# Two blocks on one core: a new engine order in the first mixer, the low-rank gate on four row groups, and gated linear attention in steps of 128 tokens

## The reference

```python
# layer 0 of the first block: HGRN2 (4 heads of 128, chunks of 32) beside a causal convolution of 31 taps
f = lb + (1.0 - lb) * sigmoid(f_pre);  k = (1.0 - lb) * sigmoid(-f_pre);  log_f = log(f)
b = cumsum(log_f within a chunk);  q_t = q * exp(b);  k_t = k * exp(-b)
o = causal(q_t k_t^T) v + q_t S;  S = exp(b_last) * S + (k * exp(b_last - b))^T v
o = rms_scaled(o) * hg_norm_g * silu(g)
u = silu(layer_norm(conv31(a * sigmoid(a_gate)) + cv_b));  y = [o, u] @ w_out
# layer 0 of the second block: gated linear attention (4 heads, keys 128, values 256, chunks of 64)
gk = log_sigmoid(glr @ w_gk2 + b_gk) / 16.0            # glr: 16 columns of the input projection
bcum = cumsum(gk within a chunk);  q_t = q * exp(bcum);  k_t = k * exp(-bcum)
o = causal(q_t k_t^T) v + q_t S;  S = exp(b_last) * S + (k * exp(b_last - bcum))^T v
o = rms_scaled(o) * g_onorm * silu(gate);  y = o @ w_out
```

## Time and profile before

| what | us |
|---|---|
| median of 3 runs | 2440.03 |
| lowest and highest | 2439.95, 2444.16 |
| the profiled execution | 2439.76 |
| its span, first to last instruction | 2437.7 |

### The profile page before, as it was taken

The page is one execution under the profiler, slowest core; times in us unless marked ns, Lnnn a source line. Parts: engine busy times, 40 slices in busy tenths (PEclk is TensorE's granted clock), DMA queues, the critical chain, the costliest instruction groups (busy, mean ns, idle before and its releaser), DMA issues.

```text
span 2437.7 us, 28654 instructions
## 1 busy us (share of the span) xinstructions
PE 2392.6 (98%) x11134; PEld 1948.9 (80%) x11134; DVE 1455.0 (60%) x2006; ACT 867.0 (36%) x1221; POOL 21.6 (1%) x36
## 2 busy tenths in 40 slices
PE   8998999999999999999999999999999999999998
PEld 7886788888887887788887786788888777888886
DVE  6987746544446845544446735565666776665566
ACT  4444544322223743322223534422222465222222
POOL 0000000000000000000000000000000000000000
PEclk9999999999999999999999999999999999999999
DMA  5222212222222211222222221234333211222221
GB/s 186 100 104 87 87 69 104 98 102 91 99 103 69 104 69 69 87 104 87 102 103 74 103 88 52 70 114 120 107 121 109 87 69 52 104 87 102 103 87 68
DMA packets 38715, 228.06 MB, mean 94 GB/s; under 512 B 8790, under 2 KB 8806, under 8 KB 12401
## 3 DMA queue, kind: packets, MB, share of 16 engines
q1 hardware_dynamic: 31680, 219.17, 25.2%
q0 software_dynamic: 6960, 7.86, 1.3%
HBM read 221.71 MB, written 5.24 MB: 93 GB/s over the span
## 4 chain that ended last, share of the span: by engine, by line
PE 87%; DVE 6%; ACT 4%; issue 1%; DMA 1%; SPq 0%; DVEq 0%; ACTq 0%
PE bank L708 86%; DVE w_lo L2059 1%; ACT w_hi L1472 1%; DMA w_raw<-weights_in 1%; ACT xh L1491 1%; ACT xs L1555 1%; DVE xl L2074 1%; DVE xs L2189 1%; PE bank L1409 1%; DVE sum_q L2088 0%; DVE xs L2169 0%; DVE cacc L2295 0%; ACT pr L1797 0%; DVE sum_x L2081 0%; DVE rmax L2498 0%
## 5 line engine op out<-in xcount | busy, mean ns | idle before, releaser
L2059 DVE TENSOR_TENSOR w_lo<-w_raw,w_hi 128x2048 fp32r<-128x2048 f32 x200 | 458.1, 2290 | 377.5 <-ACT w_hi L1472 377.3
L708 PE MATMUL bank<-xh,w_hi 128*128 128x512 f32 x1408 | 553.7, 393 | 14.5 <-DVE w_lo L2516 6.7
L708 PE MATMUL bank<-xl,w_hi 128*128 128x512 f32 x1408 | 548.9, 390 | 0.0
L708 PE MATMUL bank<-xh,w_lo 128*128 128x512 f32 x1408 | 548.9, 390 | 0.0
L1472 ACT ACTIVATE w_hi<-w_raw 128x2048 fp32r<-128x2048 f32 x200 | 381.7, 1908 | 431.3 <-PE bank L708 423.2
L2145 DVE TENSOR_TENSOR xs<-xs,bank 128x512 f32<-128x512 f32 x448 | 294.4, 683 | 102.1 <-PE bank L708 101.2
L708 PEld LDWEIGHTS bank<-xh,w_hi 128*128 128x128 f32 x1408 | 264.8, 188 | 78.7 <-DVE w_lo L2516 6.7
L708 PEld LDWEIGHTS bank<-xh,w_lo 128*128 128x128 f32 x1408 | 264.7, 188 | 55.4
L708 PEld LDWEIGHTS bank<-xl,w_hi 128*128 128x128 f32 x1408 | 264.9, 188 | 54.4 <-issue 0.5
L708 PE MATMUL bank<-yh,w_hi 128*128 128x512 f32 x576 | 227.1, 394 | 0.4 <-DVE w_lo L2059 0.3
L708 PE MATMUL bank<-yl,w_hi 128*128 128x512 f32 x576 | 224.3, 389 | 0.0
(11 more groups left out here) (299 smaller groups left out, 2876.9 us busy)
## 6 DMA issues: line engine op xcount, KB each, us to landing
w_raw<-weights_in SPq DMA_DIRECT2D x204, 1024.0 KB, 4.8
rel_scratch<-vt POOLq DMA_DIRECT2D x8, 384.0 KB, 19.9
bias<-rel_scratch POOLq DMA_DIRECT2D x8, 256.0 KB, 3.1
y_out<-xs SPq DMA_DIRECT2D x8, 256.0 KB, 2.1
xs<-x_in SPq DMA_DIRECT2D x3, 512.0 KB, 8.1
mk<-mem_in POOLq DMA_DIRECT2D x1, 1024.0 KB, 9.9
window<-consts_in POOLq DMA_DIRECT2D x1, 576.0 KB, 6.5
xs<-x_in SPq DMA_DIRECT2D x2, 256.0 KB, 4.0
```

The costliest lines, as they stand in the source:

```text
L708: return pe.matmul(dst, a, b, start=start, stop=stop)
L2059: dve.tensor_tensor(w_lo[:, slot(c), :], w_raw[:, c % 2, :], w_hi[:, slot(c), :].bitcast(F32), ALU.subtract)\
```

## The change

In the first mixer:

- ACT scales f and k by the lower bound itself, and drains g with Silu, after one more load of its function table. DVE's eight multiplications for f and four for g go.
- DVE's taps move: the first pair ends before the second `a` unit, the second pair has 17 in place of 12 ahead of the recurrence. Around the last unit of the last head `taps(8)`, split becomes `taps(3)`, split, `taps(3)`.
- In `recurrence()`, ACT's `copy_out(2h+1)` moves ahead of `round_unit(2h+3)`. PE waits for the drained v tiles in `within_chunks(0)` and no longer before `open_head(0)`.

In the second block:

- The low-rank columns are laid four times into `glr`, so that `glow` has a copy in each of four groups of 32 rows. `wgk` has head h in rows 32h to 32h+15. The four products `gkz` use the four groups, after all four waits for a free bank.
- States run over four chunks of 128: three products, three updates, three products back, each on the full array. Scores inside 128 tokens get four more products of 64x64 from `gk1`, with DVE instructions for `hde`, `gk1` and the odd halves of q (`qs_ready`). A mask of 128 is loaded by POOL.

The core of the diff:

```diff
@@ ACT, recurrence
                     if h:
                         outputs(h - 1)
+                    copy_out(2 * h + 1)
                     round_unit(2 * h + 3)
                     if h + 1 < HEADS:
                         token_keys(h + 1)
                     scaled_rows(h)
-                    copy_out(2 * h + 1)
@@ ACT, f and g
-                    act.activation(hb[:, h, :], bank(key)[:, :], ACT.Sigmoid)
+                    steps.step(act.activation(hb[:, h, :], bank(key)[:, :], ACT.Sigmoid))
                     free(act.activation(hk[:, h, :], bank(key)[:, :], ACT.Sigmoid, scale=-1.0), key)
+                    steps.wait()
+                    steps.step(act.activation(hb[:, h, :], hb[:, h, :], ACT.Identity, scale=lb1[:, h:h + 1], bias=lb0[:, h:h + 1]))
+                    wait_drained(act, key)
+                    act.activation(hk[:, h, :], hk[:, h, :], ACT.Copy, scale=lb1[:, h:h + 1])
+            act.preload_act_table_set("silu_and_others")
             for j in range(2):
                 split_hi(UNITS["g"] + j + 1)
-                for m in range(2):
...
+                drain_pair("g", j, lambda m: hg[:, 2 * j + m, :], func=ACT.Silu)
@@ DVE, taps
-                        taps(8)
+                        taps(3)
                         split_unit(2 * h + 3)
+                        taps(3)
...
-            taps(10)
+            taps(14)
             for j in range(2):
                 split_lo(UNITS["f"] + j + 1)
                 if j:
                     memory_sums()
-                taps(9)
...
+                taps(11)
             for j in range(2):
                 split_lo(UNITS["g"] + j + 1)
-                taps(9)
...
+                taps(13)
...
-            taps(12)
+            taps(17)
@@ PE, low-rank gate
             for h in range(HEADS):
                 wait_free(pe, ("gkz", h))
-                full(mm(bank(("gkz", h))[:, :], wgk[96:128, h * P:(h + 1) * P], glow[96:128, :], True, True), ("gkz", h))
+            for h in range(HEADS):
+                r = slice(32 * h, 32 * h + 32)
+                full(mm(bank(("gkz", h))[:, :], wgk[r, :], glow[r, :], True, True), ("gkz", h))
@@ PE, gated linear attention
                     for t in range(TT):
                         a = slice(t * P, (t + 1) * P)
-                        last = mm(bank(("gla", "scores", h))[:, a], gk[:, h, a], gq[:, h, a], True, True)
+                        mm(bank(("gla", "scores", h))[:, a], gk[:, h, a], gq[:, h, a], True, True)
+                    for t in range(TT):
+                        a = slice(t * P + 64, (t + 1) * P)
+                        last = mm(bank(("gla", "scores", h))[0:64, a], gk1[:, t * 64:(t + 1) * 64], gq[:, h, a], True, True)
...
-                    state_steps(h, 0)
-                    state_steps(h, 1)
+                    state_steps(h)
                     within_chunks(h, 1)
                     if h:
                         feature_major(h - 1)
-                    across_chunks(h, 0)
-                    state_steps(h, 2)
+                    seen.next("qs_ready")
                     across_chunks(h, 1)
-                    state_steps(h, 3)
                     if h + 1 < HEADS:
                         open_head(h + 1)
                     across_chunks(h, 2)
@@ DVE, gated linear attention: prepare, and the order of a head
+                    steps.step(dve.tensor_copy(hde[:, s, 0:TT], geb[:, :].rearrange("p (c e t) -> p c e t", e=2, t=64)[:, :, 0, 63]))
...
+                    steps.step(dve.tensor_tensor(two[:, :, 0], two[:, :, 0], two[:, :, 1], ALU.mult))
+                    dve.tensor_tensor(gk1[:, :].rearrange("p (c t) -> p c t", t=64),
+                                      gk[:, h, :].rearrange("p (c e t) -> p c e t", e=2, t=64)[:, :, 0, :],
+                                      hde[:, s, 0:TT].unsqueeze(2).broadcast_to([P, TT, 64]), ALU.mult)
...
-                    state_steps(h, 0)
-                    state_steps(h, 1)
+                    state_steps(h)
                     if h:
                         gated(h - 1)
-                    state_steps(h, 2)
-                    state_steps(h, 3)
-                    if h:
                         outputs(h - 1)
```

More of the change, by code:

```diff
@@ L177, in gla @@
                 fill(("gla", "o", h, 1), 7)
-                for i in range(2 * TT - 1):
-                    fill(("gla", "ds", h, i), i % 4)
+                for i in range(TT - 1):
+                    fill(("gla", "ds", h, i), i)
     def recurrence():
@@ L560, in build @@
         genb = sb(gla_mem, "genb", [P, T])
-        wgk = sb(gla_mem, "wgk", [P, HEADS * P])
+        wgk = sb(gla_mem, "wgk", [P, P])
+        gk1 = sb(gla_mem, "gk1", [P, TT * 64])
+        sb(gla_mem, "wgk_pad", [P, P])
         scan64 = sb(gla_mem, "scan64", [P, T])
@@ L979, in within_chunks, with state_steps @@
                            gv[:, t, h * 2 * P:(h + 1) * 2 * P], s == 0, False)
[L981 to L986, removed]
+                def state_steps(h):
+                    for t in range(TT - 1):
+                        key = ("gla", "ds", h, t)
                         wait_free(pe, key)
-                        r = slice(64 * c, 64 * c + 64)
-                        full(mm(bank(key)[:, 0:2 * P], kT[r, t * P:(t + 1) * P],
-                                gv[r, t, h * 2 * P:(h + 1) * 2 * P], True, True), key)
+                        full(mm(bank(key)[:, 0:2 * P], kT[:, t * P:(t + 1) * P], gv[:, t, h * 2 * P:(h + 1) * 2 * P], True, True), key)
                 def across_chunks(h, t):
                     key = ("gla", "o", h, t // 2)
[L995 to L1001, removed]
+                    wait_drained(pe, ("gla", "ds", h, t - 1))
+                    last = mm(bank(key)[:, (t % 2) * 2 * P:(t % 2 + 1) * 2 * P], gq[:, h, t * P:(t + 1) * P],
+                              gs[:, t * 2 * P:(t + 1) * 2 * P], False, t % 2 == 1)
                     if t % 2:
@@ L1862, in _ @@
             drain_pair("q", 1, lambda m: hq[:, 2 + m, :])
-            seen.next("f_ready", HEADS)
+            steps.wait()
             for h in range(HEADS):
@@ L2412, in prepare, with state_steps @@
                                            gk[:, h, :].rearrange("p (c t) -> p c t", t=64),
[L2413 to L2420, removed]
+                                           hdec[:, s, 0:8].unsqueeze(2).broadcast_to([P, 8, 64]), ALU.mult), "kq_ready")
+                def state_steps(h):
+                    for i in range(TT - 1):
                         key = ("gla", "ds", h, i)
-                        src = bank(key)[:, 0:2 * P]
-                        to = gs[:, ((i + 1) % 8) * 2 * P:((i + 1) % 8 + 1) * 2 * P]
+                        src, to = bank(key)[:, 0:2 * P], gs[:, (i + 1) * 2 * P:(i + 2) * 2 * P]
                         wait_full(dve, key)
@@ L2543, in _ @@
             steps.wait()
-            steps.step(dve.tensor_scalar(lb1[:, :], lb0[:, :], -1.0, 1.0, ALU.mult, ALU.add))
+            give(dve.tensor_scalar(lb1[:, :], lb0[:, :], -1.0, 1.0, ALU.mult, ALU.add), "lb_ready")
             split_lo(UNITS["ag0"] + 1)
@@ L2581, in _ @@
                     memory_sums()
-                taps(9)
-                for m in range(2):
-                    h = 2 * j + m
-                    wait_drained(dve, ("f", j, m))
-                    dve.tensor_scalar(hk[:, h, :], hk[:, h, :], lb1[:, h:h + 1], None, ALU.mult)
-                    give(dve.tensor_scalar(hb[:, h, :], hb[:, h, :], lb1[:, h:h + 1], lb0[:, h:h + 1], ALU.mult, ALU.add), "f_ready")
+                taps(11)
             for j in range(2):
                 split_lo(UNITS["g"] + j + 1)
-                taps(9)
-                for m in range(2):
-                    key, h = ("g", j, m), 2 * j + m
-                    seen.next("gate_ready")
-                    wait_full(dve, key)
-                    free(dve.tensor_tensor(hg[:, h, :], hg[:, h, :], bank(key)[:, :], ALU.mult), key)
+                taps(13)
             split_lo(UNITS["a1"] + 1)
```

38 lines of the change are left out of this document (23 added, 15 removed).

## The result

| what | us |
|---|---|
| after: median of 6 runs | 2426.21 (2424.69 to 2429.50) |
| before: median of 6 runs on the same chip | 2440.99 (2439.95 to 2444.16) |
| ratio | 0.9937, 95% interval 0.9927 to 0.9948 |
| profiled execution of after, its span | 2426.31, 2424.5 |

The account below looks back on a forecast made before the run. PE, busy for 98% of the span, was taken as the bound. Mixer -13.4, gate -0.2 and gated attention -1.1 sum to -14.7 us: profiled 2439.76 becomes 2425.1, median 2425.3, range 2420 to 2431.

Parts of the forecast that it names:

- Part 1: Recurrence, ACT's order: two waits go (-7.0 us) and the clock no longer falls behind them (-4.1), -11.1 us.
- The 0.2 us of room ahead of head 3: Recurrence: DVE's chain for head 3 ends at about 191.5, PE wants it at about 191.7; the tightest place.
- Part 2: Ahead of the recurrence: memory sums +0.57 us, wait for `hv` gone, head 0 starts at 142.3; net -0.5 us.
- Part 3: End of the recurrence: split no longer behind eight taps, -1.15 us; fewer taps left, 0.65 usable; -1.8 us.
- `scaled_rows(3)` ends about 0.7 after PE wants it: End of the recurrence: `copy_out(7)` ahead of ACT's rounding makes ACT late, leaving -1.15 of 1.86 us.
- Part 4: Gate: four groups fully overlap, 1.0 us for 3.70, but DVE's split binds and PE waits 2.0; -0.2 us.
- Part 5: Gated attention: ACT and DVE set the pace, `kT` to `kT` 9.96 to 9.87 us; -1.1 us in all.
- the first rival: Clock falls at new idle places, each costing up to 1.59 us; one to four give 2427 to 2432; chance 0.25.
- the stretch from 1365 to 1520: Gate through gated heads: PEclk below 1.00 anywhere in it was named a sign of the prediction being wrong.
- The rival of a PE that sets the pace: Second block: gate gives 2.6 us and each head 1.3 to 2; total 2415 to 2419; chance 0.08.
- the one of drains that don't matter: Recurrence: another wait takes the place of both long waits; total 2436 to 2440; chance 0.03.
- A clock that stays low through the gated heads: Gated heads at 1.2 GHz: +19 us, more than the 14.7 gained, so slower than before; chance 0.02.

Follow-up runs that it names:

- busy_before: Kernel before plus 14 unused matmuls on PE in each of the recurrence's two long waits; 2438.64 us, ratio 0.9982.
- mixer_only: Kernel before with all of the first mixer's changes and none of the second block's; 2430.17 us, ratio 0.9948.
- steps128_only: Kernel before with gated attention in steps of 128 alone; 2441.16 us, ratio 0.9998.
- both_moves_one_group: `both_moves` with the four `gkz` products on one row group as in the kernel before; 2424.82 us, ratio 0.9929.
- busy_one_group: `both_moves` plus nine unused products ahead of tile 4 of the first mixer's output projection, `gkz` on one row group; 2425.45 us, ratio 0.9930.
- copy_first: Kernel before with only ACT's `copy_out(2h+1)` moved ahead of `round_unit(2h+3)`; 2432.57 us, ratio 0.9961.
- gate_only: Kernel before with the low-rank gate on four row groups alone; 2440.34 us, ratio 0.9997.
- gk1_four_times: Changed kernel with DVE's `gk1` product made four times in each `prepare`, each waited for; 2431.56 us, ratio 0.9953.
- gk_split_early: Changed kernel with rounding and split of the second `gk` unit ahead of the gate's chain on ACT and DVE; 2425.93 us, ratio 0.9929.
- last_head_later: Changed kernel with the last `feature_major` behind four k-tiles of `go` in place of two; 2424.81 us, ratio 0.9924.
- both_moves: Changed kernel with the edits of `gk_split_early` and `last_head_later` together; 2422.32 us, ratio 0.9917.

## Why the prediction held, and where its steps were off

**Part 1** was right in both its terms: from the opening of the recurrence to its last `across_chunks` PE needs 66.19 us in place of 77.22, -11.0 for a forecast of -11.1, and `busy_before` splits it as the prediction did, 4.1 of it clock. The 0.2 us of room ahead of head 3 was there: between 140 and 215 us the trace has no wait of PE.

**Part 2** was worth 0.3, not 0.5. The first g unit's rounding ends at 59.0 (forecast 58.9) and the memory sums at 65.25 (65.2); PE's last sum over them starts 0.66 us later than before for a forecast of 0.57. The rest lies within what two traces differ by.

**Part 3** was mis-sized, the largest miss of the sum: 14.71 us in place of 17.37 from the last `across_chunks` to the end of the sums, -2.7 for a forecast of -1.8. The failed step is "`scaled_rows(3)` ends about 0.7 after PE wants it". ACT's chain from the drain of the last tile to the last scaled row runs from 208.76 to 213.93, and PE starts the transposes at 213.99, 0.33 behind the start of its last product, where it was 0.23 before: at most 0.1 us of wait. The prediction counted both drains of `copy_out(7)` ahead of the rounding. In the timeline of after the first runs at 206.04, while PE still works on the unit, and only the second (208.76; the rounding starts 0.50 later) is in the way. So this term gave -1.9 in place of -1.15. The taps gave 0.77 where 0.65 was forecast.

**Part 4**: the products do run fully side by side, 1.07 us from start to start, so the value taken between the bounds was right. The Trainium skill, "TensorEngine Tiling (Array Packing)", Theoretical Speedup, promises up to 4x. The trace stays a little below it: 3.63 to 1.07 is 3.4x. None of it reached the end, as the prediction had worked out from DVE's chain. PE waits 1.77 us for `w_lo` (forecast 2.0), ahead of it 0.46 for `rtok` (0.3). Net 0.0 for a forecast of -0.2. What the prediction missed is another difference between the two forms. Falls that begin in the `gkz` products or up to 0.7 us behind them stand in the traces of kernels with the one-group form alone: five such kernels show one (`mixer_only`, `busy_before`, `steps128_only`, `both_moves_one_group`, `busy_one_group`), two do not (before, `copy_first`), and of the seven kernels with four groups, `gate_only` among them, none does. These are single profiled executions, so the share is rough, and in the kernel before the effect has no measured worth: `gate_only` is at 0.9997 (0.9988 to 1.0006).

**Part 5**: `kT` to `kT` is 9.85 us for a forecast of 9.87, the wait before the last `feature_major` 2.06 for 2.2, and the whole -0.84 for -1.1. `gk1_four_times` shows why the smaller PE work is worth so little: what is added to DVE's `prepare` is added to the period in full.

**The sum** was 14.7; the traces give 14.9 up to the last `feature_major`. That close an agreement is partly luck: part 3 gave 0.9 more than forecast, and the other parts some 0.7 less together. It is 13.45 for the profiled executions as a whole, because the first rival came true once: the clock fell behind the new 2.06 us wait, for the 1.6 us it was priced at. The fall at 1518.7 also lies in the stretch from 1365 to 1520 where the prediction took any PEclk below 1.00 for a sign of being wrong; that sign was drawn too wide, as its own rival allowed such a fall. The medians differ by 14.8, as forecast, though falls come and go in both kernels (2439.95 to 2444.16 before, 2424.69 to 2429.50 after), so this too is partly luck. The rival's wording, falls at *new idle* places, was too narrow in two ways: they also come behind the old 2.0 us wait for `xl` (in five of the twelve traces that have it), and without any idle time at the one-group products. The Trainium skill, "TensorE: Matmul & The Clock Gate", Part 1: The HAM clock gate, says that the gate goes by how busy PE has been recently, and its table of the two states names idle time alone as what brings the lower one. `busy_one_group` shows a fall with no idle time in the records of PE. The rival of a PE that sets the pace fell with `gate_only` and `steps128_only`, the one of drains that don't matter with `copy_first`. A clock that stays low through the gated heads did not occur: 3.4 us behind them is all in this trace.

**Left open**: what part of the spread of the changed kernel's runs (2424.7 to 2429.5) each place has. Only profiled executions show places.

## What to carry to other kernels

Read an idle time of the bounding engine together with the clock of the stretch behind it: here 7.0 us of waits cost 11.0. An edit that shortens work on an engine that waits right behind it can be worth nothing by itself, but ask at once what it is worth after the next wait is gone: the row groups went from 0.0 to 2.0 us when the split of one unit was moved ahead of a chain. Where single events of 1.6 us come and go between executions, settle a change of 1 or 2 us by start-to-start times at fixed places of the traces and use medians as a second witness.

## What the hardware showed that was not expected

- The clock can fall during or just behind products on 32 of the 128 rows, one after another for 3.6 us, with PE busy throughout: PEclk 0.50 for 6.8 us in `mixer_only` and `busy_one_group`.
- Four float32 products of 512 columns, eight records, take 1.07 us from start to start on four row groups, where one row group takes 3.63.
- Nine unused products, 2.17 us from start to start, in a wait of 2.00 us (2.4 from start to start) did not delay the unit behind them, and the kernel's five runs agree within 0.8 us, for 2.1 us without them.
- Whether the same wait of 2.0 us for `xl` is followed by a fall differs between executions of nearly the same kernel: none in the trace of after and six others, one in those of `busy_before`, `gk_split_early`, `last_head_later`, `gk1_four_times` and `both_moves`.
